# A power of -0.5 on GpSimd in place of a square root and a reciprocal in the norms of a two-layer hybrid trunk

## The reference

```python
def layer_norm(x, g, b):
    mu = mean(x, -1)
    var = mean(square(x - mu), -1)
    return (x - mu) * rsqrt(var + 1e-5) * g + b

for i in range(2):
    # layer 0: gated DeltaNet; layer 1: short gated convolution
    mix = delta_mixer(x) if i == 0 else shortconv_mixer(x)
    x = layer_norm(ALPHA * x + mix, ln_mix_g[i], ln_mix_b[i])
    f = (silu(conv(x @ w_up)[gate]) * conv(x @ w_up)[value]) @ w_down
    x = layer_norm(ALPHA * x + f, ln_ffn_g[i], ln_ffn_b[i])
    x = x + (p[i] @ ple_w_proj[i]) * sigmoid(x @ ple_w_gate[i])

# inside delta_mixer, for each of 8 heads of width 128, ahead of the output product:
o = o * rsqrt(mean(o * o, -1) + 1e-6) * norm_g * silu(z)
```

## Time and profile before

| what | value |
|---|---|
| time, median of 2 runs | 1886.7 us (1885.82 to 1887.59) |
| profiled execution | 1885.29 us, of which the span is 1883.5 us |
| PE busy | 1802.9 us, 96% |
| DVE busy | 1158.2 us, 61% |
| ACT busy | 461.5 us, 25% |
| POOL busy | 261.0 us, 14% |
| mean granted clock of TensorE | 0.984 |

### The profile page before, as it was taken

One profiled execution on the slowest core, in us unless ns is written; L12 is line 12 of the kernel. 1 busy time (PEld: TensorE's weight loads), 2 busy tenths in 40 slices (PEclk: granted clock), 3 DMA queues, 4 the chain that ended last, 5 costly groups with the idle time before them and its releaser, 6 DMA issues. The chain is left out here.

```text
span 1883.5 us, 22711 instructions
## 1 busy us (share of the span) xinstructions
PE 1802.9 (96%) x7821; PEld 1399.4 (74%) x7821; DVE 1158.2 (61%) x2236; ACT 461.5 (25%) x1069; POOL 261.0 (14%) x554
## 2 busy tenths in 40 slices
PE   7999998998898999999999999999799999999999
PEld 4777677898476777777777677776577777777767
DVE  3756576675867767666333665546776666653365
ACT  1433412552213222222001411111322222210041
POOL 0111002326123000000011100001410000001120
PEclk9999999997999999999999999999999999999999
DMA  4211111002410212223213022220122222332121
GB/s 155 77 68 68 64 34 45 1 0 102 156 44 27 86 68 90 68 88 140 78 62 107 18 90 90 88 79 24 45 83 74 79 79 79 97 122 91 54 72 51
DMA packets 44455, 138.48 MB, mean 74 GB/s; under 512 B 4792, under 2 KB 12088, under 8 KB 44224
## 3 DMA queue, kind: packets, MB, share of 16 engines
q1 hardware_dynamic: 42704, 134.60, 20.7%
q10 hardware_dynamic: 1648, 2.56, 0.4%
HBM read 128.85 MB, written 8.29 MB: 73 GB/s over the span
## 5 line engine op out<-in xcount | busy, mean ns | idle before, releaser
L267 PE MATMUL bank<-z,ring 128*128 128x288 f32 x1952 | 511.3, 409 | 6.2 <-DVE z L365 3.4
L267 PEld LDWEIGHTS bank<-z,ring 128*128 128x128 f32 x1952 | 372.9, 191 | 113.5 <-issue 4.1
L267 PE MATMUL bank<-x,ring 128*128 128x288 f32 x1632 | 431.7, 412 | 16.6 <-DMA ring<-in_w_qkv 6.6
L267 PEld LDWEIGHTS bank<-x,ring 128*128 128x128 f32 x1632 | 313.1, 193 | 110.2 <-issue 12.4
L1948 DVE SCALAR_TENSOR_TENSOR scratch<-scratch 128x592 f32<-128x592 f32 x176 | 146.1, 831 | 25.5 <-ACT scratch L1892 23.8
L267 PE MATMUL bank<-y,ring 128*128 128x288 f32 x616 | 156.6, 406 | 1.0 <-ACT z L2012 0.5
L267 PE MATMUL bank<-big,ring 128*128 128x288 f32 x536 | 136.6, 410 | 5.9 <-issue 5.1
L267 PEld LDWEIGHTS bank<-y,ring 128*128 128x128 f32 x616 | 116.8, 190 | 34.1 <-ACT z L2012 1.0
L267 PEld LDWEIGHTS bank<-big,ring 128*128 128x128 f32 x536 | 102.2, 191 | 36.4 <-issue 7.4
L1892 ACT ACTIVATE scratch<-scratch 128x592 f32<-128x592 f32 x88 | 69.4, 789 | 91.3 <-DVE scratch L1922 89.8
L1982 POOL COPY scratch<-scratch 128x2 f32<-128x2 f32 x88 | 26.4, 301 | 462.2 <-ACT scratch L1878 462.2
(11 more groups left out here) (343 smaller groups left out, 2482.3 us busy)
## 6 DMA issues: line engine op xcount, KB each, us to landing
ring<-in_w_up SPq DMA_DIRECT2D x88, 512.0 KB, 3.5
ring<-in_w_qkv SPq DMA_DIRECT2D x24, 512.0 KB, 3.5
ring<-in_w_scin SPq DMA_DIRECT2D x24, 512.0 KB, 3.4
ring<-in_w_down SPq DMA_DIRECT2D x12, 704.0 KB, 4.0
scratch<-in_w_down SPq DMA_DIRECT2D x12, 704.0 KB, 4.7
ring<-in_w_z SPq DMA_DIRECT2D x8, 512.0 KB, 3.4
big<-in_st_S SPq DMA_DIRECT2D x16, 256.0 KB, 5.7
out_dn_S_sample<-big SPq DMA_DIRECT2D x16, 256.0 KB, 2.0
```

The source lines that it names most:

```text
L267: last = pe.matmul(bank[:, 0:HALF], w[:, k * P:(k + 1) * P], rhs(k), start=start and k == 0, stop=k == self.depth - 1, skip_group_check=no ...
```

## The change

The four LayerNorms and the RMS norm get their inverse deviation by one elementwise power with the exponent -0.5 on GpSimd. `variance` adds 1e-5 in the instruction that clips at zero. `inverse` moves from VectorE's queue to GpSimd's, where it stands ahead of `centre_pool`; `deviation` goes. In the RMS norm ScalarE only scales and adds the constant (Identity), GpSimd does two powers on 8 partitions in a row, and TensorE waits for both of ScalarE's results ahead of its 16 products. The exponent is a column of constants, spread over the 288 columns, that GpSimd fills once.

```diff
-            def deviation(self, act, half):
-                act.wait_ge(ln_var, 2 * at + 2)
-                act.activation(rs[:, cols], rs[:, cols], ACT.Sqrt, bias=eps_ln).then_inc(ln_std, 1)
...
-                dve.tensor_scalar(rs[:, cols], rs[:, cols], 0.0, None, ALU.max).then_inc(ln_var, 1)
-            def inverse(self, dve, half):
-                dve.wait_ge(ln_std, at + 1)
-                dve.reciprocal(rs[:, cols], rs[:, cols]).then_inc(ln_inverse, 1)
+                dve.tensor_scalar(rs[:, cols], rs[:, cols], 0.0, 1e-5, ALU.max, ALU.add).then_inc(ln_var, 1)
+            def inverse(self, pool, half):
+                pool.wait_ge(ln_var, 2 * at + 2)
+                pool.tensor_tensor(rs[:, cols], rs[:, cols], neg_half.to_broadcast([P, HALF]), ALU.pow
+                                   ).then_inc(ln_inverse, 1)
... GatedNorm
+                pe.wait_ge(self.std, 2)
-                                   ACT.Sqrt, bias=eps_rms[0:H], scale=1.0 / P).then_inc(self.std, 1)
+                                   ACT.Identity, bias=eps_rms[0:H], scale=1.0 / P).then_inc(self.std, 1)
             def pool(self, pool):
                 pool.memset(self.rstd, 0.0).then_inc(self.clr, 1)
+                pool.memset(neg_half, -0.5).then_inc(self.clr, 1)
+                pool.wait_ge(self.clr, 2)
+                for half in range(2):
+                    cols = slice(half * HALF, (half + 1) * HALF)
+                    pool.wait_ge(self.std, half + 1)
+                    pool.tensor_tensor(self.rstd[0:H, cols], self.rstd[0:H, cols],
+                                       neg_half[0:H].to_broadcast([H, HALF]), ALU.pow).then_inc(self.rec, 1)
-                dve.wait_ge(self.std, 2)
-                for half in range(2):
-                    dve.reciprocal(self.rstd[0:H, cols], self.rstd[0:H, cols]).then_inc(self.rec, 1)
... the calls: n.deviation and n.inverse leave ScalarE's and VectorE's orders; GpSimd's get
+            n.inverse(pool, 0)                      # mixer_pool, down_pool
             n.centre_pool(pool, 0, slice(2, 5))
+            norm[2 * layer].inverse(pool, 1)        # up_pool
             norm[2 * layer].centre_pool(pool, 1, slice(2, 8))
+                norm[1].inverse(pool, 1)            # and norm[3], behind down_pool
                 norm[1].centre_pool(pool, 1, slice(2, 8))
```

More of the change, by code:

```diff
@@ L1514, in build @@
         scaled, squared, sq_added, y_added = (phase_sem(f"res_{x}") for x in ("scaled", "squared", "sq_added", "y_added"))
-        ln_sums, ln_mean, ln_var, ln_std, ln_inverse, ln_centred, ln_centred_dve, ln_scaled, ln_ready = (
-            phase_sem(f"ln_{x}") for x in ("sums", "mean", "var", "std", "inverse", "centred", "centred_dve", "scaled",
+        ln_sums, ln_mean, ln_var, ln_inverse, ln_centred, ln_centred_dve, ln_scaled, ln_ready = (
+            phase_sem(f"ln_{x}") for x in ("sums", "mean", "var", "inverse", "centred", "centred_dve", "scaled",
                                      "ready"))
+        neg_half = CV[:, 159:160]
         samples_in, hist_in, tap0_done, tap1_done, conv_done, silu_done, gated, saved, pads, state_in = (
@@ L1719, in mean @@
                 act.activation(mu[:, cols], BANK[6][:, 0:HALF], ACT.Copy, scale=1.0 / D).then_inc(ln_mean, 1)
-            def deviation(self, act, half):
-                at, cols = 2 * self.number + half, slice(half * HALF, (half + 1) * HALF)
-                act.wait_ge(ln_var, 2 * at + 2)
-                act.activation(rs[:, cols], rs[:, cols], ACT.Sqrt, bias=eps_ln).then_inc(ln_std, 1)
             def affine(self, act, half, m):
@@ L1831, in gate @@
                                              op1=ALU.mult).then_inc(self.gated, 1)
-                dve.wait_ge(self.std, 2)
-                for half in range(2):
-                    cols = slice(half * HALF, (half + 1) * HALF)
-                    dve.reciprocal(self.rstd[0:H, cols], self.rstd[0:H, cols]).then_inc(self.rec, 1)
                 dve.wait_ge(self.gated, H)
@@ L2418, in residual_act @@
             n.mean(act, 0)
-            n.deviation(act, 0)
             r.square(act, 10)
@@ L2433, in up_act @@
             f.copy_s1(act, 1)
-            n.deviation(act, 1)
             for m in n.ORDER[1]:
@@ L2636, in down_dve @@
             n.centre_dve(dve, 0)
-            n.inverse(dve, 0)
             n.scale(dve, 0, slice(0, None))
@@ L2707, in second_half_dve @@
             n.centre_dve(dve, 1)
-            n.inverse(dve, 1)
             n.scale(dve, 1, slice(0, 4))
@@ L2880, in down_pool @@
                 r.add_piece(pool, x)
+            n.inverse(pool, 0)
             n.centre_pool(pool, 0, slice(2, 8))
@@ L3059, in _ @@
                 down_pool(pool, 1)
+                norm[3].inverse(pool, 1)
                 norm[3].centre_pool(pool, 1, slice(2, 8))
```

## The result

The changed kernel takes 2337.3 us (median of 2 runs, 2336.6 to 2338.0) against 1886.7: ratio 1.239, 95% interval 1.237 to 1.241, so 451 us slower. The profiled execution took 2336.6 us with a span of 2334.5. The forecast was 1937 us with a range up to 2070: the sign was right, the size was not.

The account below looks back on a forecast made before the run. TensorE, busy 96% of the span, was taken as the bound, so only its waits count. Chains of 41.6 us at P = 7 plus 8.7 us of clock, +50.3, gave 1937 us; range 1876 to 2070.

Parts of the forecast that it names:

- The price P: Duration of one GpSimd power on 128x288: taken as 7 us, lower bound 0.84 us, upper bound 21 us.
- The chains: At each norm, variance, power, GpSimd's subtractions and VectorE's scales become one chain, where root, reciprocal and subtractions ran side by side.
- The formula: All nine places: 8P - 20.9 plus the larger of P - 2.6 and 2P - 7.5; 41.6 us at P = 7.
- clock term: Longer TensorE waits lower its clock, 2.9 us a place: three places, 8.7 us, taken; five at most, 14.5 us.
- the break-even: The P at which a place ends as late as now: 2.35 to 2.8 us in LayerNorm halves.
- Rival 1: The power is cheap, P under 2.6 us, and the kernel faster: 1872 us at a plain operation's price; chance 0.18.
- Table loads worth nothing: ScalarE's four square-root table loads, 1.28 us each, go, but earn nothing since other work hides them.
- The power's equal length on 8 partitions: RMS norm: each of its two powers on 8 partitions takes as long as one on 128.
- VectorE's 19 us: Time freed on VectorE by the removed reciprocals earns nothing beyond the sum, since VectorE would wait for GpSimd.
- rival 4: The slips don't add: VectorE catches up and half of the 50 us comes back, 1912 us; chance 0.03.
- Rival 3: The power is long, over 12 us: at 17 us, with five clock falls, 2043 us; chance 0.22.
- The threshold of 2%: 37.7 us, about what a measurement can tell from no change; reached at P = 6 with two clock falls.

Follow-up runs that it names:

- the multiplication: The changed kernel with a multiplication by the same column in place of the power at all ten places: 1877.6 us, ratio 0.9962 to the kernel before.

## Why the prediction was wrong

**The price P failed, and with it the time and the range.** The forecast took two iterated parts at VectorE's price for a reciprocal, times the ratio of the engines, 7.1 us, and called 21 us (25 plain steps) the upper end. Measured: 46.4 us, 6.6 times the estimate and 2.2 times the bound. The error was to read a price from rows of another engine and another function, and then to take a number of steps for a bound that no row supported. What GpSimd does in those 46.4 us, steps or something else, no run shows. The text itself said that nothing in the trace bounds the steps; the chance of 0.22 for "over 12 us" was right in kind, but the range should have been open above that, as each microsecond of P is worth 8 to 10. The 2.9 us estimated from the Trainium skill, "GPSIMD Engine Reference", section 3.1, are further off still, and its factor of 2 for elementwise work (section 4.1) holds for the multiplication (0.81 us against 0.38), not for a power; there the measurement decides.

**The chains held in the main.** The formula at the measured P gives 435.6 us and the clock up to 14.5. Place by place, with the measured P (us):

| place | forecast | chain, measured | from | PE's slip |
|---|---|---|---|---|
| mixer norms, first half, two | 43.7 each | 43.7 and 43.5 | variance to bank read, 53.52 and 53.35 against 9.85 | 43.7, 43.5 |
| mixer norms, second half, two | 44.0 each | 45.7 and 45.5 | variance to token, 52.60 against 6.92 and 7.06 | 44.9, 44.9 |
| down norms, first half, two | 43.6 each | 44.1 each | variance to bank read, 53.34 against 9.25 | 45.3, 45.8 |
| down norms, second half, two | 43.8 each | 45.7 each | PE's wait, 46.9 against 1.2 | 47.5, 48.6 |
| RMS norm | 85.3 | | | 86.3 |

PE's slip is read by laying the two traces' 7821 products side by side. The product that starts at 553.11 us before norm 0's first half starts at 638.62 in the changed kernel, the one at 572.53 behind it at 701.73, so this place costs 43.7 us. In the mixers' second halves the slip is less than the chain, since the clock was down there in the kernel before too (0.59 from 587 to 594 us, 0.57 from 1347 to 1351). The slips sum to 450.4 of 451 us, so no place was missed. They are 14.8 us more than the formula's 435.6, and the forecast's clock term was 14.5. That the two agree is in part luck: the chains alone, 358.0 us in the LayerNorms for 350.3, account for 7.7 of it, and only the other half is left to the clock and to what else changes behind the waits.

**The term that was mis-sized there** is the time of VectorE's scales beside POOL's pieces: 0.98 us for 0.38. In the second halves the break-even is 0.7 to 0.8 us for it, not 2.35 and 2.6; in the first halves it is 2.7 to 2.9 and 2.3, against 2.7 and 2.8. It made the small-P side of the forecast too good: the true sum at the price of a plain operation is -7 us (measured), not -15. Rival 1 was right in its sign and half in its size.

**Table loads worth nothing**: shown (ratio 0.9998). The comparison of norm 0 and norm 2 in the earlier trace rows pointed the right way. It is shown with the kernel's own queues only; what the loads cost with the subtractions on VectorE no run shows.

**Each of the other items.** The power's equal length on 8 partitions: shown (46.49 and 46.38 us). VectorE's 19 us earn nothing beyond the sum: borne out in that the slips added up and rival 4 fell, and with the multiplication the gain was below the sum, 7 us of 15. Rival 3, a long power, was the case, at 2.7 times its price. The clock: it is down behind all ten waits of the changed kernel, and in the trace before it is down behind three of the nine (RMS norm, norm 0's second half, norm 1's first), so six are new where the forecast had five at most. PE is busy for 1815.8 - 1802.9 = 12.9 us longer with the same products, but part of that fills waits that were there before, and less than 8 us of it can be in the time. The 2.9 us a fall was too much. The threshold of 2% was called about what a measurement can tell; the runs told 3 us of 1887 from nothing (1.0008 to 1.0025).

## What to carry to other kernels

Before an elementwise function goes to an engine on which the trace has never shown it, run one instruction of it: an estimate by likeness with another engine was off by a factor of 6.6 here, and a range built on such likeness is no range. An operation priced by the column is worst on data that is alike in all partitions, as here the inverse deviation: 288 columns on 128 partitions cost the same as on 8. (Spreading the 288 values over the partitions was not run.) When a forecast's sum comes out right, lay the traces side by side and compare it term by term: here one term was short by what another had too much. And help from GpSimd counts only after the loss on VectorE is taken off: 48 subtractions moved back to VectorE cost 3 us in place of 18, and with ScalarE's inverse root they made the fastest kernel, 1863.9 us, 1.2% under the kernel before.

## What the runs showed of the hardware

A power on GpSimd takes 0.16 us a column for float32, with under 1 us for the instruction, whatever the exponent (-1 or -0.5) and for 8 as for 128 partitions; a multiplication in the same form takes 0.81 us in all. A two-input VectorE operation on 128x288 takes 0.38 us from start to start alone and 0.98 us beside GpSimd's two-input operations. Those go from 0.84 us (six in 5.06 us, beside little of VectorE's work) to 0.94 and 0.98 us (six in 5.62 in the changed kernel and in 5.85 with the multiplication). TensorE's granted clock is 0.50 or 0.51 at the start of the products behind each of ten waits of 39.6 to 48.9 us. ScalarE's Abs_reciprocal_sqrt takes the same 0.53 us as its square root and replaces root and reciprocal.
